# The norm between two layers made inside the first pass of a convolution's input product

## The chip, the cores and the metric

The kernel runs on one core of one Trainium2 chip. The metric is device time in microseconds of one execution, from the first instruction to the last; smaller is better. Engines are named as in the profile: PE is TensorE (matmul), PEld its weight loads, DVE is VectorE, ACT is ScalarE, POOL is GpSimd, SP is SyncE, which here only issues transfers.

## The reference

A network of two layers works on 4096 tokens of width 1024. Layer 0 mixes tokens by a state space model, layer 1 by a short convolution; each is followed by a mixture of experts. What lies around the change is the start of layer 1:

```
hn = modulate(rmsnorm(x, norm1_g[1]), sh1, sc1)       # x * rsqrt(mean(x*x) + eps) * g * (1 + sc1) + sh1
b_g, c_g, v = split(hn @ w_in, 3)                     # w_in 1024 x 3072
u = c_g * v
z = causal depthwise convolution of u, 3 taps
out = (b_g * z) @ w_out
```

The scale and shift belong to a channel, the root mean square to a token.

## The kernel before

The program is a row of phases with a barrier between them. `finish_layer` (tag `c0`) makes the norm between the layers and `conv_in` (tag `conv`) the first product and the convolution; `project` (tag `cout`) and the experts follow. `finish_layer` with tag `c1` makes the final norm at the end.

`finish_layer` takes 32 tiles of 128 tokens. SP loads a tile of x (512 KB, L1845) four deep; ACT squares and sums it (L1878) and takes the root (L1880); DVE takes the reciprocal (L1925), multiplies by it and by the gain (L1930) and adds the shift (L1932), all over 1024 channels with gain and shift broadcast to 128 partitions; PE transposes eight squares of 128 x 128 (L1906); ACT copies them out of PSUM (L1888); POOL stores them into `hnT`, channels by tokens (L1869).

`conv_in` needs products that are as exact as fp32 from the faster fp32r form, so each operand is split into a high part (ACT, a copy that rounds to fp32r) and a low part (DVE, raw minus high), and `product` (L127 to L129) makes three matmuls: weight high by x low, low by high, high by high. Four passes c each take a quarter of the output channels (2 x 128 for each of B, C and V), with their weights held in SBUF. In each pass 8 blocks of 512 tokens follow. A block has two halves m, each with three groups n (C, V, B) of 8 k x 3 matmuls of 128 x 128 by 128 x 512 into a PSUM bank: 48 groups in a pass, 192 in all. SP loads a block of x from `hnT` (2 MB, L1973) as soon as the buffer's block before is done, ACT splits (L2006, two instructions for a block), DVE subtracts (L2070). ACT also copies C out of its bank (L2023), DVE multiplies by V (L2093), applies the taps (L2097 to L2100) and gates with B (L2103), and POOL stores the result to `zT` (L2051). The weights of the next pass (8 transfers of 384 KB, L1970) are split at the start of a pass, ahead of everything else on ACT (L1997) and DVE (L2063). PE's waits are: the weights of the pass, the low part of the block, and for each half m that DVE has read that half's banks (`used`). Six of eight PSUM banks are in use.

All four passes run as hardware loops over pairs of blocks. Each engine's order is the program's; semaphores count up and waits are on counts.

Of the kernel before, what the change touches and what calls it, by code (L numbers as in the profile page):

```python
# [24 lines left out]
F32 = mybir.dt.float32  # L25
# [6 lines left out]
P = 128  # L32
D = 1024
# [1782 lines left out]
def finish_layer(core, ident, tag, layer, x1_dram, mod_dram, gain_src, hnT_dram=None, out=None):  # L1816

    nc = core.nc
    last_layer = out is not None
    W = 8 if last_layer else 4  # L1820
# [4 lines left out]
    tp, t_out, t_st = sem("transposed"), sem("hT_out"), sem("hT_stored", W)  # L1825
    with ExitStack() as ctx:
        sb = lambda name, shape, dt=F32: core.sb(ctx, f"{tag}_{name}", shape, dt)
        sbs = lambda name, n, shape, dt=F32: core.sbs(ctx, f"{tag}_{name}", n, shape, dt)
        gain, shift, scale = sb("gain", [P, D]), sb("shift", [P, D]), sb("scale", [P, D])
        xb, hn = sbs("x", W, [P, D]), sbs("hn", W, [P, D])  # L1830
        junk = sb("junk", [P, D])
        hT = None if last_layer else sbs("hT", W, [P, KD, P])
        eps, stat = sb("eps", [P, 1]), sbs("stat", W, [P, 4])
        pT = None if last_layer else [core.ps(ctx, f"{tag}_pT{s}", [P, KD, P]) for s in range(W)]
        block = ctx.enter_context(nc.Block())
        x1_view = x1_dram[0:T, :].rearrange("(n p) d -> n p d", p=P)
        if last_layer:
            out_view = out.rearrange("b (n p) d -> n p (b d)", p=P)
        else:
            hT_view = hnT_dram.rearrange("(k p) (n f) -> n p k f", p=P, f=P)  # L1840

        @block.sync
        def _(sp):
            def load(n):
                sp.dma_start(xb[n % W][:], x1_view[n]).then_inc(x_ld[n % W], 16)  # L1845
# [4 lines left out]
            if not last_layer:  # L1850
                load_mod(sp, mod_dram, layer + 1, SC1, scale[:], const_ld)
                load_mod(sp, mod_dram, layer + 1, SH1, shift[:], const_ld)
            for n in range(2, W):
                load(n)
            for n in range(NT):
                if n + W < NT:
                    sp.wait_ge(hn_ready, n + 1)
                    load(n + W)

        @block.gpsimd  # L1860
        def _(pool):
            for n in range(NT):
                s = n % W
                if last_layer:
                    pool.wait_ge(hn_ready, n + 1)
                    pool.dma_start(out_view[n], hn[s][:]).then_inc(o_st[s], 16)  # L1866
                else:
                    pool.wait_ge(t_out, n + 1)
                    pool.dma_start(hT_view[n], hT[s][:]).then_inc(t_st[s], 16)  # L1869
            for s in range(W):  # L1870
                pool.wait_ge(o_st[s] if last_layer else t_st[s], 16 * (NT // W))

        @block.scalar
        def _(act):
            def std_of(n):
# [7 lines left out]
            def out_t(n):  # L1883
                s = n % W
                act.wait_ge(tp, n + 1)
                if n >= W:
                    act.wait_ge(t_st[s], 16 * (n // W))
                act.activation(hT[s][:], pT[s][:], ACT.Copy).then_inc(t_out, 1)  # L1888

            act.wait_ge(eps_set, 1)  # L1890
            for n in range(NT + 2):
                if n < NT:
                    std_of(n)
                if n >= 2 and not last_layer:
                    out_t(n - 2)

        if not last_layer:
            @block.tensor
            def _(pe):
                for n in range(NT):  # L1900
                    s = n % W
                    pe.wait_ge(hn_ready, n + 1)
                    if n >= W:
                        pe.wait_ge(t_out, n - W + 1)
                    for k in range(KD):
                        last = pe.transpose(pT[s][:, k, :], hn[s][:, k * P:(k + 1) * P], ident[:])  # L1906
                    last.then_inc(tp, 1)

        @block.vector
        def _(dve):  # L1910
            c = Chain(dve, step)
            dve.memset(eps[:], EPS).then_inc(eps_set, 1)
            dve.wait_ge(const_ld, 16 if last_layer else 48)
            if not last_layer:
                fold_scale(dve, c, gain[:], scale[:])
            stt, tt = dve.scalar_tensor_tensor, dve.tensor_tensor
            for n in range(NT):
                s = n % W
                dve.wait_ge(std, n + 1)
                if n >= W:  # L1920
                    if last_layer:
                        dve.wait_ge(o_st[s], 16 * (n // W))
                    else:
                        dve.wait_ge(tp, n - W + 1)
                c(dve.reciprocal(stat[s][:, 2:3], stat[s][:, 1:2]))  # L1925
                if last_layer:
                    stt(out=hn[s][:], in0=xb[s][:], scalar=stat[s][:, 2:3], in1=gain[:],  # L1927
                        op0=ALU.mult, op1=ALU.mult).then_inc(hn_ready, 1)
                else:
                    c(stt(out=hn[s][:], in0=xb[s][:], scalar=stat[s][:, 2:3], in1=gain[:],  # L1930
                          op0=ALU.mult, op1=ALU.mult))
                    tt(hn[s][:], hn[s][:], shift[:], ALU.add).then_inc(hn_ready, 1)  # L1932
# [4 lines left out]
def conv_in(core, tag, w_in, conv_w, hnT_dram, z_dram):  # L1937
# [5 lines left out]
    TB = T // HALF  # L1943
# [3 lines left out]
    r_ld, r_hi, r_lo = sem("r_loaded", 2), sem("r_hi"), sem("r_split")  # L1947
    mm, c_out, used, step = sem("bank"), sem("c_out"), sem("banks_read"), sem("dve_step")
    z_ready, z_go, z_st = sem("z_ready"), sem("z_stores"), sem("z_stored", 2)
    with ExitStack() as ctx:  # L1950
# [3 lines left out]
        x_raw, x_lo = zip(*[core.raw_low(ctx, f"{tag}_x{s}", [P, KD, HALF]) for s in range(2)])  # L1954
        w_hi, x_hi = sbs("w_hi", 2, [P, KD, 3, W], F32R), sbs("x_hi", 2, [P, KD, HALF], F32R)
        taps = sb("taps", [P, 3, NC_ * MC])
        u = sbs("u", 2, [P, MC, HALF + 2])
        cs = sbs("c", MC, [P, HALF])
        z = sbs("z", MC, [P, HALF])
        pb = [[core.ps(ctx, f"{tag}_p{j}_{m}", [P, HALF]) for j in range(3)] for m in range(MC)]  # L1960
        block = ctx.enter_context(nc.Block())
        w_view = w_in[0].rearrange("(k p) (j c f) -> c p k j f", p=P, j=3, f=W)
        x_view = hnT_dram.rearrange("(k p) (n f) -> n p k f", p=P, f=HALF)
# [3 lines left out]
        def _(sp):  # L1967
# [4 lines left out]
            def load(r, t, s):  # L1972
                sp.dma_start(x_raw[s][:], x_view[bass.ds(t, 1)].squeeze(0)).then_inc(r_ld[s], 16)  # L1973

            sp.dma_start(taps[:], conv_w[0].rearrange("j (c p) -> p j c", p=P), allow_slow_non_contiguous=True) \
              .then_inc(cw_ld, 16)
            weights(0)
            for s in range(2):
                load(0, s, s)
            for c in range(NC_):  # L1980
                if c + 1 < NC_:
                    if c >= 1:
                        sp.wait_ge(mm, 3 * MC * TB * c)
                    weights(c + 1)
                last = c == NC_ - 1
                with sp.Fori(0, TB // 2 - (1 if last else 0)) as i:
                    for s in range(2):
                        b = c * TB + 2 * i + s
                        sp.wait_ge(mm, 3 * MC * (b + 1))
                        load(None, (2 * i + s + 2) % TB, s)  # L1990

        @block.scalar
        def _(act):
            def split_w(c):
                for k in range(KD):
                    act.wait_ge(w_ld[c % 2][k], 16 * (c // 2 + 1))
                    act.activation(w_hi[c % 2][:, k, :, :], w_raw[c % 2][:, k, :, :], ACT.Copy) \  # L1997
                       .then_inc(w_hi_r, 1)

            def split_x(c, i, s):  # L2000
# [172 lines left out]
```

## Time and profile before

| | us |
|---|---|
| median of 3 runs | 7090.4 |
| lowest, highest | 7086.16, 7091.12 |
| the profiled execution, its time | 7087.8 |
| the profiled execution, its span | 7085.8 |

The profiled execution is one execution with the hardware profiler on. Its span is from the first to the last instruction in the trace; its time is 2.0 us longer. Instruction counts, durations and idle times of the profile belong to it alone. The page gives busy shares of the engines over the span, a strip of 40 slices, the queues and the costliest groups of instructions; the trace behind it answers questions on stretches and on single instructions, with times in us from the start of the span. Matmuls are pipelined: a duration of 0.39 us of a 128 x 512 matmul holds its passage through the array, and the rate is read from the distance of two starts.

### The profile page before, as it was taken

To read this page: it belongs to the slowest core of one execution; us is meant where nothing else is said; L and a number is where in the kernel's file an instruction comes from. 1 tells how busy PE (TensorE), PEld (TensorE's weight loads), DVE (VectorE), ACT (ScalarE), POOL (GpSimd) and SP (SyncE) were. 2 spreads that over 40 slices of the span, in tenths; PEclk is the share of its full clock that TensorE was granted. 3 is DMA by queue.
4 is the path that set the end of the run, shared out by engine and by line. 5 is a ranking of instruction groups with operands and counts; after the bars stand their busy time and mean duration, and the time that the engine had idled before them with its cause. 6 is when DMAs were issued, how large, how long until landed. Compare 5 with 4: busy or idle time off the path is not lost. (4 is left out here: it accounts for less than half of the span.)

```text
span 7085.8 us, 90556 instructions
## 1 busy us (share of the span) xinstructions
PE 6435.3 (91%) x30729; PEld 5259.4 (74%) x30730; DVE 3486.6 (49%) x4917; ACT 2114.6 (30%) x3269; POOL 1486.9 (21%) x1278
## 2 busy tenths in 40 slices
PE   6997888799995999999995999998998599999994
PEld 2876766588884888888884888887777488888883
DVE  4435666344336564555646333433544744556554
ACT  1112444222221343343425111111111233344434
POOL 0001221587002222222321000000000322222222
PEclk8998999899997999999995999999998899999997
DMA  6221111444222676676747222221433465677766
GB/s 202 66 85 45 60 51 46 153 145 142 83 80 101 187 225 178 201 213 201 213 131 269 74 94 97 84 87 66 155 130 116 134 193 165 187 215 238 221 201 246
DMA packets 502953, 1024.21 MB, mean 145 GB/s; under 512 B 62526, under 2 KB 140350, under 8 KB 501834
## 3 DMA queue, kind: packets, MB, share of 16 engines
q1 hardware_dynamic: 395604, 740.36, 30.7%
q0 software_dynamic: 74336, 265.88, 14.5%
q10 hardware_dynamic: 32920, 16.80, 0.8%
q8 instruction: 50, 0.82, 0.0%
q14 instruction: 43, 0.35, 0.0%
HBM read 784.34 MB, written 238.60 MB: 144 GB/s over the span
## 5 line engine op out<-in xcount | busy, mean ns | idle before, releaser
L127 PE MATMUL conv_p<-conv_x_lo,conv_w_hi 128*128 128x512 f32 x1536 | 598.7, 390 | 33.0 <-DVE conv_x_lo L2070 33.0
L128 PE MATMUL conv_p<-conv_x_hi,conv_w_lo 128*128 128x512 f32 x1536 | 598.5, 390 | 0.0
L129 PE MATMUL conv_p<-conv_x_hi,conv_w_hi 128*128 128x512 f32 x1536 | 598.5, 390 | 0.0
L1758 DVE SCALAR_TENSOR_TENSOR m_o<-m_pO,m_weight_of,m_gate 128x512 f32<-128x512 f32 x320 | 237.8, 747 | 723.9 <-PE m_pO L1478 404.4
L1725 DVE TENSOR_TENSOR m_w_lo<-m_w_raw,m_w_hi 128x1024 fp32r<-128x1024 f32 x496 | 577.6, 1214 | 0.0
L1533 ACT ACTIVATE m_xT_hi<-m_pX 128x512 fp32r<-128x512 f32 x320 | 191.6, 599 | 1151.9 <-PE m_pB L129 994.2
L127 PE MATMUL m_pA<-m_w_lo,m_xT_hi 128*128 128x512 f32 x1280 | 517.2, 404 | 5.7 <-DVE m_xT_lo L1736 5.7
L1474 PE MATMUL m_pO<-m_w_lo,m_hT_hi 128*128 128x512 f32 x1280 | 512.8, 401 | 0.5 <-ACT m_hT_hi L1538 0.5
L1521 ACT ACTIVATE m_w_hi<-m_w_raw 128x1024 fp32r<-128x1024 f32 x512 | 505.3, 1053 | 0.0
L129 PE MATMUL m_pA<-m_w_hi,m_xT_hi 128*128 128x512 f32 x1280 | 502.9, 393 | 0.0
L128 PE MATMUL m_pA<-m_w_hi,m_xT_lo 128*128 128x512 f32 x1280 | 500.2, 391 | 0.0
L1474 PE MATMUL m_pO<-m_w_hi,m_hT_hi 128*128 128x512 f32 x1280 | 498.9, 390 | 0.0
L127 PE MATMUL m_pB<-m_w_lo,m_xT_hi 128*128 128x512 f32 x1280 | 498.1, 389 | 0.0
L129 PE MATMUL m_pB<-m_w_hi,m_xT_hi 128*128 128x512 f32 x1280 | 498.0, 389 | 0.0
L128 PE MATMUL m_pB<-m_w_hi,m_xT_lo 128*128 128x512 f32 x1280 | 497.9, 389 | 0.0
L1383 POOL COPY m_gather_now<-m_gather_of 128x1 int32 (+1 forms) x164 | 186.7, 1138 | 1162.6 <-DMA x<-m_o,m_scatter_now 874.2
L127 PE MATMUL glu_pM<-glu_w_lo,glu_sT_hi 128*128 128x512 f32 x1024 | 405.9, 396 | 12.1 <-DVE glu_w_lo L1111 12.1
L129 PE MATMUL glu_pM<-glu_w_hi,glu_sT_hi 128*128 128x512 f32 x1024 | 401.6, 392 | 0.0
L128 PE MATMUL glu_pM<-glu_w_hi,glu_sT_lo 128*128 128x512 f32 x1024 | 401.5, 392 | 0.0
L127 PEld LDWEIGHTS conv_p<-conv_x_lo,conv_w_hi 128*128 128x128 f32 x1536 | 289.0, 188 | 93.5 <-issue 33.4
L1731 DVE TENSOR_TENSOR m_w_lo<-m_w_raw,m_w_hi 128x1024 fp32r<-128x1024 f32 x256 | 306.2, 1218 | 86.3 <-issue 65.6
L1478 PE MATMUL m_pO<-m_w_hi,m_hT_lo 128*128 128x512 f32 x1280 | 342.1, 389 | 0.0
(346 smaller groups left out, 13001.3 us busy)
## 6 DMA issues: line engine op xcount, KB each, us to landing
m_w_raw<-in_moe_w_dram SPq DMA_DIRECT2D x384, 1024.0 KB, 7.2
conv_x_raw<-hnT SPq DMA_DIRECT2D x32, 2048.0 KB, 9.3
c_x<-x SPq DMA_DIRECT2D x64, 512.0 KB, 7.5
mod_w<-in_ada_w_dram SPq DMA_DIRECT2D x12, 2048.0 KB, 7.9
glu_ada<-in_ada_w_dram POOLq DMA_DIRECT2D x96, 256.0 KB, 3.2
a_x<-in_x_dram SPq DMA_DIRECT2D x32, 512.0 KB, 3.5
u<-a_stage POOLq DMA_DIRECT2D x4, 4096.0 KB, 19.1
s_u<-u SPq DMA_DIRECT2D x64, 256.0 KB, 2.6
```

The costliest lines, as they stand in the source:

```text
L127: pe.matmul(out, lh, rl, start=start, stop=False)
L128: pe.matmul(out, ll, rh, start=False, stop=False)
L129: return pe.matmul(out, lh, rh, start=False, stop=stop)
L1383: pool.tensor_copy(gx[:], gidx[:, bass.ds(t, 1)]).then_inc(gi_ready, 1)
L1474: pe.matmul(pO[:, n, :], hT_hi[:, k, :], w[:, n, k, :], start=k == 0 and w is w2_low, stop=False)
L1478: last = pe.matmul(pO[:, n, :], hT_lo[:, k, :], w2_high[:, n, k, :], start=False, stop=k == KF - 1)
L1521: act.activation(W13[s][2][:, m, k:k + 2, :], W13[s][0][:, m, k:k + 2, :], ACT.Copy).then_inc(w13_hi, 1)
L1533: act.activation(xT_hi[:, 4 * q:4 * q + 4, :], pX[:, 4 * q:4 * q + 4, :], ACT.Copy).then_inc(xt_hi, 1)
L1725: tt(W13[s][1][:, m, k:k + 2, :], W13[s][0][:, m, k:k + 2, :], W13[s][2][:, m, k:k + 2, :].bitcast(F32), ALU.subtract).then_inc(w13_lo, 1)
L1731: tt(w2_low[:, n, k:k + 2, :], w2_raw[:, n, k:k + 2, :], w2_high[:, n, k:k + 2, :].bitcast(F32), ALU.subtract).then_inc(w2_lo, 1)
L1758: dve.scalar_tensor_tensor(out=ob[:, n, :], in0=pO[:, n, :], scalar=wslot[:, bass.ds(tile_, 1)], in1=gate2[:, n, :], op0=ALU.mult, op1=ALU ...
```

## The change

`finish_layer` keeps only the final norm, under the name `final_norm`; its work at the end of the program is as before. The phase `c0` and the tensor `hnT` are gone. `conv_in` now gets x, the gain and the row of modulation, and its pass 0 is written out without a loop:

- SP loads the four 128-token tiles of block 0, then the weights of pass 0. For each block b it waits until the block is transposed, loads the tiles of block b + 1 into the same four buffers, waits for the low parts, and stores high and low part (2 x 2 MB) to two tensors in DRAM. The weights of pass 1 go out behind the stores of block 0.
- Gain, scale, shift (1024 numbers each, laid out 8 to a partition) and taps are loaded from POOL's queue; DVE folds the gain once.
- ACT makes square sum and root of a tile; DVE takes the reciprocal and multiplies the tile in place (`scaled`), without gain and shift.
- PE transposes 4 squares of 128 x 128 into one of the two PSUM banks that were free (`turned`), for block 0 all eight k ahead of the products, for block b + 1 two k behind each of the first four groups of block b.
- ACT reads the bank with an affine copy, with gain and shift as its per-partition operands, into `xt` (`x_high`), then rounds it into the high part; DVE subtracts (`x_low`).
- Passes 1 to 3 load high and low part of a block ready (two transfers of 2 MB instead of one), and ACT and DVE split no x there. PE waits for the loads themselves.

The core of the diff:

```diff
+            def load(t, s):
+                for part, dst in zip(hT_view, (x_hi[s], x_lo[s])):
+                    sp.dma_start(dst[:].bitcast(F32), part[bass.ds(t, 1)].squeeze(0)).then_inc(r_ld[s], 16)
+            for j in range(TPB):
+                sp.dma_start(rows[j][:], x_view[j]).then_inc(n_ld[j], 16)
             weights(0)
+            for b in range(TB):
+                sp.wait_ge(t_psum, KD * (b + 1))
+                if b + 1 < TB:
+                    for j in range(TPB):
+                        sp.dma_start(rows[j][:], x_view[TPB * (b + 1) + j]).then_inc(n_ld[j], 16)
+                sp.wait_ge(r_lo, KD * (b + 1))
+                for part, src in zip(hT_view, (x_hi[b % 2], x_lo[b % 2])):
+                    sp.dma_start(part[b], src[:].bitcast(F32)).then_inc(r_st[b % 2], 16)
+                if b == 0:
+                    weights(1)
             for s in range(2):
-                load(0, s, s)
+                sp.wait_ge(r_st[s], 32 * (TB // 2))
+            for s in range(2):
+                sp.wait_ge(mm, GROUPS * (TB - 1 + s))
+                load(s, s)
...
+            def x_high(b, k):
+                n = KD * b + k
+                act.wait_ge(t_psum, n + 1)
+                if n >= 2:
+                    act.wait_ge(r_lo, n - 1)
+                act.activation(xt[n % 2][:], pT[n % 2][:], ACT.Identity, scale=gains[:, 0, k:k + 1],
+                               bias=gains[:, 2, k:k + 1]).then_inc(t_out, 1)
+                act.wait_ge(t_out, n + 1)
...
+                act.activation(x_hi[b % 2][:, k, :], xt[n % 2][:], ACT.Copy).then_inc(r_hi, 1)
...
+            for n in range(TPB):
+                std_of(n)
+            act.wait_ge(gain_ready, 1)
+            for k in range(KD):
+                x_high(0, k)
+                w_high(0, k)
+            for n in range(TPB, 2 * TPB):
+                std_of(n)
+            for b in range(TB):
+                c_copy(b, 0)
+                if b + 1 < TB:
+                    for k in range(6):
+                        x_high(b + 1, k)
+                c_copy(b, 1)
+                if b + 1 < TB:
+                    for k in range(6, KD):
+                        x_high(b + 1, k)
+                if b + 2 < TB:
+                    for n in range(TPB * (b + 2), TPB * (b + 3)):
+                        std_of(n)
...
+            def turned(b, k):
+                n = KD * b + k
+                if k == 0:
+                    pe.wait_ge(n_ready, TPB * (b + 1))
+                if n >= 2:
+                    pe.wait_ge(t_out, n - 1)
+                for j in range(TPB):
+                    last = pe.transpose(pT[n % 2][:, j * P:(j + 1) * P], rows[j][:, k * P:(k + 1) * P], ident[:])
+                last.then_inc(t_psum, 1)
...
+            for k in range(KD):
+                turned(0, k)
+            for b in range(TB):
+                pe.wait_ge(r_lo, KD * (b + 1)) if b else None
+                for m in range(MC):
+                    pe.wait_ge(used, MC * b + 1 + m)
+                    for n in range(3):
+                        group(0, b % 2, m, n, b + m + n == 0)
+                        if b + 1 < TB and 3 * m + n < 4:
+                            turned(b + 1, 2 * (3 * m + n))
+                            turned(b + 1, 2 * (3 * m + n) + 1)
...
+            for b in range(TB):
+                q = lambda m: Chain(dve, step, base_of(0) + 1 + (b * MC + m) * per)
+                more = b + 1 < TB
+                for k in range(2 if more else 0):
+                    x_low(b + 1, k)
+                taps_of(0, b, b % 2, 0, q(0))
+                for k in range(2, 4 if more else 2):
+                    x_low(b + 1, k)
+                gated(b, 0)
+                for k in range(4, KD if more else 4):
+                    x_low(b + 1, k)
+                taps_of(0, b, b % 2, 1, q(1))
+                gated(b, 1)
+                if b + 2 < TB:
+                    for n in range(TPB * (b + 2), TPB * (b + 3)):
+                        scaled(n)
+                if b == 1:
+                    for k in range(KD):
+                        w_low(1, k)
```

`scaled(n)` is a reciprocal of 128 x 1 and a `tensor_scalar` multiply of 128 x 1024 in place, with the reciprocal as its per-partition operand. `taps_of` and `gated` hold the instructions of L2093 to L2103. `group` holds the loop over k of `product`.

## Rows read from the trace of the kernel before

**Rows 1.** The profile's page, part 1: engine, busy us, share of span, instructions.
```profile
PE 6435.3 (91%) x30729; PEld 5259.4 (74%) x30730; DVE 3486.6 (49%) x4917; ACT 2114.6 (30%) x3269; POOL 1486.9 (21%) x1278
```

**Rows 2.** Table of stretches around the change; columns as its first line says.
```profile
core 0: us, PE busy (x) PEld busy (x) DVE busy (x) ACT busy (x) POOL busy (x), PEclk, DMA share, GB/s
3757.40:3866.00 108.60, 62.98 (x256) 50.19 (x256) 84.36 (x98) 77.20 (x129) 28.52 (x32) 0.50 0.87 324
3866.00:3891.10 25.10, 0.00 (x0) 0.00 (x0) 12.16 (x10) 10.90 (x11) 0.00 (x0) 0.50 1.00 331
3891.10:4154.90 263.80, 263.78 (x1153) 218.20 (x1154) 98.77 (x120) 44.60 (x40) 8.14 (x15) 0.99 0.23 79
4154.90:4938.20 783.30, 783.30 (x3457) 648.43 (x3455) 286.33 (x353) 124.75 (x110) 25.95 (x48) 1.00 0.25 86
```

**Rows 3.** Groups by line from 3745 to 3900: busy us, mean ns | idle before.
```profile
L1932 DVE TENSOR_TENSOR c_hn<-c_hn,c_shift 128x1024 f32<-128x1024 f32 x32 | 39.2, 1225 | 1.1
L1869 POOL DMA_DIRECT2D hnT<-c_hT x32 | 28.5, 891 | 82.6 <-ACT c_hT L1888 82.6
L1925 DVE RECIPROCAL c_stat<-c_stat 128x1 f32<-128x1 f32 x32 | 5.0, 157 | 2.3 <-ACT c_stat L1880 2.3
```

**Rows 4.** The same table, the first products of pass 0 alone.
```profile
3891.10:3896.40 5.30, 5.28 (x12) 4.18 (x13) 4.62 (x5) 4.41 (x6) 0.00 (x0) 0.50 1.08 380
```

**Rows 5.** Timeline of the norm phase's start.
```profile
3761.12 1.06 ACT L1878 ACTIVATE c_junk<-c_x 128x1024 f32<-128x1024 f32 x1 [21.04 <-DMA c_x<-x]
3762.08 0.19 ACT L1878 ACTIVATION_READ_ACCUMULATOR c_junk<-c_x 128x1 f32 x1
...
3763.58 0.29 ACT L1880 ACTIVATE c_stat<-c_stat,c_eps 128x1 f32<-128x1 f32 x1
...
3771.21 1.97 PE L1906 MATMUL c_pT<-ident,c_hn 128*128 128x128 f32 x8 [25.63 <-DVE c_hn L1932]
```

**Rows 6.** Transfers by line: count, KB of each, median us to landing.
```profile
conv_x_raw<-hnT SPq DMA_DIRECT2D x32, 2048.0 KB, 9.3
...
u<-a_stage POOLq DMA_DIRECT2D x4, 4096.0 KB, 19.1
...
conv_taps<-in_conv_w_dram SPq DMA_DIRECT2D x1, 12.0 KB, 3.6
```

**Rows 7.** Single lines of DVE: ns min/median/max, first and last start us.
```profile
L1068 DVE TENSOR_SCALAR cout_gate<-cout_gate x1: 693/693/693, 4961.1 to 4961.1; 128x1024 f32<-128x1024 f32 x1
...
L2097 DVE TENSOR_SCALAR conv_z<-conv_u,conv_taps x64: 485/486/490, 3905.9 to 4933.9; 128x512 f32<-128x512 f32 x64
L2070 DVE TENSOR_TENSOR conv_x_lo<-conv_x_raw,conv_x_hi x64: 2282/2288/2294, 3886.5 to 4886.8; 128x2048 fp32r<-128x2048 f32 x64
...
L2103 DVE TENSOR_TENSOR conv_z<-conv_z,conv_p x64: 686/687/689, 3910.3 to 4938.5; 128x512 f32<-128x512 f32 x64
```

**Rows 8.** ACT's groups by form, whole span: rounding copies from SBUF.
```profile
L1140 ACT ACTIVATE cout_sT_hi<-cout_src 128x512 fp32r<-128x512 f32 x64 | 36.8, 622 | 36.2 <-DMA cout_src<-zT 33.3 <-issue 2.8
L1997 ACT ACTIVATE conv_w_hi<-conv_w_raw 128x768 fp32r<-128x768 f32 x32 | 27.1, 846 | 62.5 <-DMA conv_w_raw<-in_conv_w_in_dram 61.9
```

**Rows 9.** Timeline of PE in the expert layer, eight transposes between products.
```profile
3689.39 1.03 PE L1435 MATMUL m_pX<-ident,m_rows 128*128 128x128 f32 x8
3690.18 0.48 PE L1474 MATMUL m_pO<-m_w_lo,m_hT_hi 128*128 128x512 f32 x1
3690.50 0.40 PE L1474 MATMUL m_pO<-m_w_hi,m_hT_hi 128*128 128x512 f32 x1
```

**Rows 10.** Table of stretches, 45 us of the expert layer.
```profile
3690.00:3735.00 45.00, 43.70 (x206) 36.05 (x205) 14.58 (x22) 9.12 (x15) 7.98 (x12) 1.00 0.26 59
```

**Rows 11.** Timeline of DVE in the first block of pass 1: its first gating.
```profile
4183.16 0.69 DVE L2103 TENSOR_TENSOR conv_z<-conv_z,conv_p 128x512 f32<-128x512 f32 x1
```

**Rows 12.** Timeline of PE in `cout`: a wait of 1.1 us, then slow products.
```profile
5105.95 1.98 PE L1222 MATMUL cout_pH<-cout_router,cout_hT 128*128 128x36 f32 x16 [1.11 <-ACT cout_hT L1158]
...
5108.84 0.63 PE L127 MATMUL cout_pM<-cout_w_lo,cout_sT_hi 128*128 128x512 f32 x1
```

More of the change, by code:

```diff
@@ L1849, in _ @@
             sp.dma_start(gain[:], row(gain_src, 0, D)).then_inc(const_ld, 16)
-            if not last_layer:
-                load_mod(sp, mod_dram, layer + 1, SC1, scale[:], const_ld)
-                load_mod(sp, mod_dram, layer + 1, SH1, shift[:], const_ld)
             for n in range(2, W):
                 load(n)
[L1855 to L1858, printed above, removed]
+            for n in range(NT - W):
+                sp.wait_ge(hn_ready, n + 1)
+                load(n + W)
         @block.gpsimd
@@ L1881, in std_of @@
                    .then_inc(std, 1)
[L1883 to L1907, printed above, removed]
         @block.vector
@@ L1912, in _ @@
             dve.memset(eps[:], EPS).then_inc(eps_set, 1)
[L1913 to L1916, printed above, removed]
+            dve.wait_ge(const_ld, 16)
             for n in range(NT):
@@ L1920, in _, with conv_in @@
                 if n >= W:
[L1921 to L1924, printed above, removed]
+                    dve.wait_ge(o_st[s], 16 * (n // W))
                 c(dve.reciprocal(stat[s][:, 2:3], stat[s][:, 1:2]))
[L1926 to L1937, printed above, removed]
+                dve.scalar_tensor_tensor(out=hn[s][:], in0=xb[s][:], scalar=stat[s][:, 2:3], in1=gain[:],
+                                         op0=ALU.mult, op1=ALU.mult).then_inc(hn_ready, 1)
+def conv_in(core, ident, tag, x_dram, norm_g, mod_row, w_in, conv_w, hT_dram, z_dram):
     nc = core.nc
@@ L1942, in conv_in @@
     W = P * MC
-    TB = T // HALF
+    TB, TPB = T // HALF, HALF // P
+    GROUPS = 3 * MC
     sem = lambda name, n=None: core.sem(f"{tag}_{name}", n)
@@ new lines, in group @@
+            def group(c, s, m, n, first=False):
+                j, cols = (1, 2, 0)[n], slice(m * P, (m + 1) * P)
+                for k in range(KD):
+                    if first:
+                        pe.wait_ge(r_lo, k + 1)
+                        pe.wait_ge(w_split, k + 1)
+                    last = product(pe, pb[m][n][:], (w_hi[c % 2][:, k, j, cols], w_lo[c % 2][:, k, j, cols]),
+                                   (x_hi[s][:, k, :], x_lo[s][:, k, :]), k == 0, k == KD - 1)
+                last.then_inc(mm, 1)
@@ new lines, in _ @@
+            for k in range(KD):
+                turned(0, k)
[8 more added lines that the diff above has]
+                            turned(b + 1, 2 * (3 * m + n) + 1)
@@ L2029, in _ @@
+            for c in range(1, NC_):
                 pe.wait_ge(w_split, KD * (c + 1))
```

235 lines of the change are left out of this document (121 added, 114 removed).

## The prediction

> **What bounds the kernel now.** I read the summary first, then the table of stretches, then the timelines at the joints. TensorE is busy for 91% of the span, so the kernel ends when TensorE's stream ends, and what can be won lies where that stream has a hole or runs slowly [rows 1]. The stretches show one such hole around the change. From 3757.4 us to 3891.1 no product of the convolution runs: the norm phase takes 108.6 us (256 transposes at the low clock, 0.50), the start of `conv_in` another 25.1 us with TensorE idle. From 3891.1 to 4938.2 TensorE is busy for 1047.1 us of 1047.1 [rows 2]. The norm phase keeps DVE busy for 84.4 of its 108.6 us; the adding of the shift alone takes 1225 ns for each of 32 tiles [rows 2, 3]. Downstream nothing changes, so each microsecond by which the convolution's last product moves is one of the end.
>
> In the convolution four passes of 8 blocks make 48 groups of 24 matmuls each. Passes 1 to 3 take 783.3 us, so a group takes 783.3/144 = 5.44 us and a block of six 32.6 us; pass 0 takes 263.8 us, 2.5 us more, because its first 12 matmuls run at the low clock (0.50, which is 1.2 GHz) with starts 5.3/12, over 0.43 us apart, where a later one takes 783.3/3456 = 0.23 [rows 2, 4].
>
> **What is removed.** The norm phase as a whole (TensorE transposes, ScalarE's copies, the 32 stores, the constants broadcast to 128 partitions), one phase change, and the splits of x in passes 1 to 3 (two instructions of 128x2048 each of ScalarE and DVE in a block; 2.29 us for one of DVE [rows 7]). ScalarE and DVE are idle most of the time there [rows 2], so those splits give nothing by themselves. The gain is the hole of 3891.1 - 3757.4 = 133.7 us, less what the new start needs, less what is put into TensorE's stream.
>
> **The new start.** The phase begins at 3757.4 as before. ScalarE began on the first 512 KB of x 3.7 us into the phase (that is how long its landing took), and the transfers of that time moved 324 GB/s, thus 1.6 us for each 512 KB [rows 2, 5]. The four tiles of block 0 are there by 3765.9, now ahead of all else on SP's queue. ScalarE has the first deviation at 3763.9, table load included, and takes 1.06 + 0.19 + 0.29 us for each further one [rows 5]: the fourth at 3768.4. The small loads of gain, scale and shift are moved to POOL's queue; three issues of at most 0.9 us, the price of a 1024-run issue there [rows 3], and a landing of 3.6 us, that of the taps [rows 6], put them at 3764, hidden behind the norm. DVE scales the fourth tile by 3769.4, four transposes at 0.25 us each (1.97 us for eight at the low clock [rows 5]) end at 3770.4. Now ScalarE is the bound: for each of the 8 k it makes the affine copy and the high part (0.62 each, a copy of the same length) and a weight's high part (0.85) [rows 8], with gaps 2.2 us. TensorE stands with all eight transposes before its first product, and the last of them waits for the affine copy of k = 5, at 3782.1; products begin at 3783.1. The first 12 run at 0.43 us (3788.2), the other 12 at 0.23 us, ending at 3790.9; the last low part of a weight is ready at 3789.1 and costs nothing.
>
> Then a **bubble**. The rows of block 1 can be loaded only when block 0 is transposed (3783.1): they land from 3786.8 to 3791.6. ScalarE, free at 3788.1, has their fourth deviation at 3794.3, DVE the scaled tile at 3795.3, and TensorE's next instruction, the first transpose of block 1, waits for that from 3790.9: 4.4 us. Behind it in the same queue stand the other five groups of block 0. After it I charge one more slow start, 2.4 us. Block 0 ends at 3795.3 + 5 x 5.44 + 3.5 (its transposes, below) + 2.4 = 3828.4.
>
> **Transposes in the stream.** A block's 32 come in four slots of eight, and in the expert layer eight transposes stand between products just so: they start at 3689.39, the next product at 3690.18 and its follower 0.32 us on instead of 0.23 [rows 9]. That is 0.79 + 0.09 = 0.88 us for a slot and 3.5 us for a block, at full clock (1.00 over 45 us that hold two such slots [rows 10]). The bounds are 0.79 and, at the low clock, 1.97 us [rows 5]. Seven blocks cost 24.6 us, 3.5 of them already in block 0. TensorE's wait for a bank of k - 2 costs nothing, as ScalarE empties it in 0.6 us and a group lies between.
>
> **Does the norm keep up in pass 0?** A block has 36.1 us. ScalarE needs 8 x 1.3 + 4 x 1.55 + 2 x 0.6 = 17.8 us, DVE 8 x 0.69 [rows 7] + 4 x 1.0 + 2 x 3.7 (the gap-free run of taps and gating) = 16.9 us; neither is the bound by amount. The order leaves two places to look at. At a block's start T, DVE must finish the last gating (T + 1.0, from its 0.69 us and start 0.3 us after the last product [rows 7]), then scale four tiles before the transposes at T + 5.44. A scaling is a reciprocal of 0.16 us and a TENSOR_SCALAR with a pointer over 1024 elements. No row has that one. Bounds are 0.69 us (same length, constant operand) and 1.23 us (TENSOR_TENSOR, same length); the row of the same kind has 486 ns for 512 elements, and the 1024-element constant form has 693 [rows 3, 7], which makes 486 + 267 = 0.75 us, near the lower end. Then four end at T + 5.0, with 0.4 us to spare. The rows of the next block are issued two groups before T and land by T - 2, free of the stores of the block before. The second place is the end: the last transposes are at T + 25.4, and 0.6 + 2 x 1.3 + 0.7 us later the block's parts are ready, 7 us early.
>
> By the Trainium skill, VectorE: DVE Perf Modes, section Mode 2×_2P, a single-source operation on SBUF makes two fp32 results a cycle and tensor_tensor can't; 1225 against 693 ns in the rows agrees. If a pointer scalar lost that mode, each block would start 1.5 us late, the case given below from rows alone.
>
> **Stores and loads.** The two parts (4 MB a block) are stored on SP's queue behind the next rows; 4 MB on a queue landed in 19.1 us once [rows 6], against 36 us of a block. From pass 1 on two transfers of 2 MB replace one, which landed in 9.3 us [rows 6]: at most 18.6 us of the 32.6 that lie between issue and use. The seam of pass 0 and 1 is tighter. The parts of block 7 are stored from 29 us after block 6 begins, done 19.1 us later, 12 us into block 7; the load of block 8 behind it ends at most 18.6 us on, 2 us before use. At the seams where weights(2) and weights(3) are loaded, ScalarE waits for them and the copies of C queue behind. Before, pass 0 ended at 4154.9 and the first gating of the new pass at 4183.9, 29.0 us into a block of 32.6 [rows 2, 11]. Now 2 MB more stand ahead (at most +7.3 us, the 9.3 of such a load [rows 6] less some 2 for its reaction), but the splits of x ahead of the first gating are gone, between 4.6 us (two of 2.29) and 5.4: about 31 us. No wait, with 1.6 us to spare.
>
> **Sum.** Block 0 ends at 3828.4; blocks 1 to 6 take 6 x 36.16 = 217.0, block 7 32.6: 4078.0. Passes 1 to 3, 783.3: 4861.3 instead of 4938.2, 76.9 us sooner. The profiled execution has a span of 7085.8 and a time of 7087.8 us, thus 7008.9 and 7010.9; the median of the three runs, 7090.4, lies 2.6 us above it, and I predict 7013.5, rounded **7014 us**.
>
> **Rivals.** (1) *The norm comes late at each block*: with 1.23 us for the scaling the fourth is ready at T + 6.9, a wait of 1.5 us in six blocks, and where TensorE had waited 1.1 us once and then ran 16 small matmuls, its clock fell and the next nine product starts were 0.35 to 0.43 us apart instead of 0.23, some 1.8 us lost (one of the nine stands in the rows, with 0.63 us for 0.39) [rows 12]. 6 x 3.3 = 20 us: **7034**. For it: the margin is only 0.4 us; against it: the 486 ns row. 15%. (2) *A shorter start*: no bubble and no second slow start, 6.8 us, and the cheaper slot, 2.5 us: **7005**. 5%. (3) *No change, the norm isn't hidden after all*: if each of seven blocks waited 11 us, the gain of 76.9 would be gone: **7090**. Nothing in the amounts above speaks for that, only the handshakes of four engines. 3%. (4) *Slower, through the clock*: the many short waits between slots keep TensorE at 1.2 GHz in pass 0. A group then takes 24 x 0.427 = 10.2 us, 4.8 more; from 16 of the 48 groups on the change loses, and with all 48 it costs 230 us: **7244** at the worst, some 7110 with 20. For it: the clock that fell after a single short wait [rows 12]; against it: full clock with such slots in the expert layer [rows 10]. 5%. The forecast has 70%.
>
> (5) *Reading the code*: pass 0 is now written out, 2816 matmuls and weight loads of TensorE without a loop, and reading them might stall, which no row of a written-out stretch of this length can rule out. By the Trainium skill, Runtime: NRT & Kernel Launch, section Instruction fetch mechanics, a straight stream is fetched ahead in blocks of 256 instructions and it is taken branches that stall; that would cost nothing here. The trace shows no loss at the old loop's branches either (783.3 of 783.3 us busy [rows 2]). Were each of the eight blocks to wait once for a small landing, 3.6 us [rows 6], and then lose 1.8 us to the clock [rows 12], 43 us would go: **7057**, which I give 2%.
>
> **Chances and range.** Faster by over 0.2% (14 us, about what a measurement of this kernel can tell from no change): 0.70 + 0.15 + 0.05 + 0.02, thus 0.92; same 0.03; slower 0.05. The range reaches from rival (2), less 3 us, to rival (1) and some 10 us for a late seam or dearer slots: 7001 to 7045.
>
> **What would show it.** Right: first product near 3783, one wait of TensorE of 3 to 6 us behind the first group for DVE's scaled rows and none in blocks 2 to 7, a scaling of 0.75 us, slots of 0.88 us, pass 0 over near 4078, passes 1 to 3 in 783 us, granted clock 1.00 from block 1 on. Wrong: waits of the transposes at each block, a product waiting for loaded parts in pass 1, a clock under 1.00 inside pass 0, or TensorE idle for "issue".

## The result and the profile after

| | before | after |
|---|---|---|
| median, us | 7089.17 (4 runs) | 7015.77 (4 runs) |
| lowest, highest | 7086.16, 7091.12 | 7012.22, 7019.38 |
| profiled execution, span | 7085.8 | 7013.7 |

The ratio is 0.9897, 95% interval 0.9885 to 0.9908: 73.4 us less, where 76.9 were forecast, and 7015.8 where 7014 was predicted. (The forecast started from 7090.4, the median of three of the four runs.)

First the table of stretches of the changed kernel, from the end of its first block: start:end, length, busy time of PE, PEld, DVE, ACT and POOL with counts, granted clock, DMA share, GB/s.

```profile
3831.40:4048.70 217.30, 217.30 (x1057) 182.09 (x1057) 102.15 (x176) 104.78 (x176) 6.51 (x12) 1.00 0.51 187
4081.00:4864.70 783.70, 783.70 (x3459) 648.98 (x3457) 185.22 (x307) 41.91 (x64) 26.04 (x48) 1.00 0.40 147
```

The first line is blocks 1 to 6 with the norm in them, the second passes 1 to 3. TensorE is busy for the whole of both at clock 1.00; the second answers the last of [rows 2], with ScalarE's busy time down from 124.8 to 41.9 us and DVE's from 286 to 185, and takes as long as before. The list of TensorE's waits over both confirms it: from 3786 to 4870 it has two entries (columns: waiting instruction, releaser, us in total, times, longest).

```profile
PE conv_pT L2035 <- DVE conv_rows L2104: 5.6, 1, 5.6
PE conv_pT L2035 <- ACT conv_xt L1980: 0.9, 1, 0.9
```

Only the first lies between products; the second is the last wait of the prologue. The timeline of TensorE there (start us, duration, engine, line, instruction, idle before):

```profile
3785.63 1.11 PE L2035 MATMUL conv_pT<-ident,conv_rows 128*128 128x128 f32 x4 [0.94 <-ACT conv_xt L1980]
3786.40 0.78 PE L127 MATMUL conv_p<-conv_x_lo,conv_w_hi 128*128 128x512 f32 x1
...
3792.86 0.39 PE L129 MATMUL conv_p<-conv_x_hi,conv_w_hi 128*128 128x512 f32 x1
3798.89 1.97 PE L2035 MATMUL conv_pT<-ident,conv_rows 128*128 128x128 f32 x8 [5.64 <-DVE conv_rows L2104]
...
3836.67 0.39 PE L129 MATMUL conv_p<-conv_x_hi,conv_w_hi 128*128 128x512 f32 x1
3836.90 1.03 PE L2035 MATMUL conv_pT<-ident,conv_rows 128*128 128x128 f32 x8
3837.69 0.48 PE L127 MATMUL conv_p<-conv_x_lo,conv_w_hi 128*128 128x512 f32 x1
3838.01 0.40 PE L128 MATMUL conv_p<-conv_x_hi,conv_w_lo 128*128 128x512 f32 x1
```

The bubble stands behind the first group, and a slot of eight transposes looks in its times exactly as in the expert layer [rows 9]. ScalarE in the prologue, one k:

```profile
3770.76 1.06 ACT L1971 ACTIVATE conv_junk<-conv_rows 128x1024 f32<-128x1024 f32 x1 [1.52 <-DMA conv_rows<-x]
...
3776.57 0.76 ACT L1980 ACTIVATE conv_xt<-conv_pT,conv_gains 128x512 f32<-128x512 f32 x1
3777.36 0.63 ACT L1986 ACTIVATE conv_x_hi<-conv_xt 128x512 fp32r<-128x512 f32 x1
3777.90 0.83 ACT L1966 ACTIVATE conv_w_hi<-conv_w_raw 128x768 fp32r<-128x768 f32 x1
```

Its period is 2.06 us a k; the first line is the square sum of the fourth tile, which came late.

**Where the time went.** The phase starts at 3757.43 before and at 3759.72 after; over all profiled runs of this study with the new `conv_in` it starts between 3756.3 and 3760.9, though nothing ahead of it was changed. So the convolution is best measured from its phase's start. The last gating starts at 4938.49 before and 4864.94 after, 1181.1 and 1105.2 us into the stretch: 75.8 us less (forecast 76.9). The later start took 2.3 us back, and what follows the last product is 1.4 us longer. That part too moves without a cause in the change: from the last k's first product to the end it took 2148.3 us before, 2149.6 after, and between 2149.8 and 2153.1 in the profiled runs below that change nothing in it; `parts_alone`, which has the old norm phase, is one of them with 2151.5.

In all experiments the numbers "products begin" and "last k" (the start of the last product of line 127) are counted in us from the start of the phase; for the changed kernel they are 26.7 and 1104.3.

### The profile page after: what moved, and what is told of

Same layout as the page of the kernel before. It is cut to its first block and busy times, and to the rows that moved or that the text cites. A ratio compares the mean times of both kernels' runs of the same rounds, so it can differ in the third digit from the quotient of the medians.

```text
span 7013.7 us, 90561 instructions
## 1 busy us (share of the span) xinstructions
PE 6407.3 (91%) x30729; PEld 5236.7 (75%) x30730; DVE 3326.9 (47%) x4885; ACT 2051.1 (29%) x3301; POOL 1448.3 (21%) x1250
## 5 line engine op out<-in xcount | busy, mean ns | idle before, releaser
L129 PEld LDWEIGHTS conv_p<-conv_x_hi,conv_w_hi 128*128 128x128 f32 x1536 | 288.9, 188 | 59.9
```

What stands on the lines that cost most here:

```text
L129: return pe.matmul(out, lh, rh, start=False, stop=stop)
```

## The experiments

### One part alone: ready parts without the hidden norm

SP stores both parts in pass 0 (first hunk) and loads them in passes 1 to 3 (second hunk, with the condition under which x is still split); pass 0 splits x as before, only the others no longer do; `finish_layer` stays.

```diff
+            for b in range(TB):
+                s = b % 2
+                sp.wait_ge(r_lo, 2 * b + 2)
+                for part, src in zip(hT_view, (x_hi[s], x_lo[s])):
+                    sp.dma_start(part[b], src[:].bitcast(F32)).then_inc(r_st[s], 16)
...
+                        parts((2 * i + s + 2) % TB, s)
...
-                        if not (c == NC_ - 1 and last and s == 1):
+                        if c == 0 and not (last and s == 1):
                             split_x(c, *at(i, s, 1))
```

> One part of the change alone: the norm stays a phase of its own as in the kernel before, pass 0 of the convolution splits x as before and stores both parts, passes 1 to 3 load them ready. Theory (the whole gain is the hidden norm): TensorE was busy all through those passes, so nothing moves, 7089 +- 4 us. Rival (the ready parts relieve ScalarE and DVE and carry some of the gain): under 7080. Rival (4 MB for a block and the stores cost something): over 7095.

Measured: 7091.25 us against 7088.66, ratio 1.0004 (0.9995 to 1.0013). The table of its stretches:

```profile
3866.00:3891.50 25.50, 0.00 (x0) 0.00 (x0) 12.15 (x10) 10.86 (x11) 0.00 (x0) 0.50 1.01 335
3891.50:4155.00 263.50, 263.48 (x1153) 218.00 (x1154) 94.36 (x118) 41.02 (x38) 8.15 (x15) 0.99 0.57 214
4155.00:4938.00 783.00, 783.00 (x3456) 648.31 (x3455) 185.12 (x307) 41.91 (x64) 25.95 (x48) 1.00 0.40 147
```

DVE is relieved by the same 100 us as in the changed kernel and the pass takes the same 783 us. The last k starts 1180.1 us after the norm phase's start in both traces. The ready parts bring nothing and cost nothing here. What they are for is room: with them passes 1 to 3 need neither norm nor transposes. The other half, a hidden norm whose result is split again in every pass, was not run.

### What the transposes cost in the stream

```diff
-                for j in range(TPB):
+                for j in list(range(TPB)) * (2 if b else 1):
                     last = pe.transpose(pT[n % 2][:, j * P:(j + 1) * P], rows[j][:, k * P:(k + 1) * P], ident[:])
```

> The changed kernel with every transpose of blocks 1 to 7 made twice into the same place (the same values). Theory (the transposes stand in TensorE's stream at full clock and cost what they take): 28 slots of eight more at 0.79 us, 22 us, time near 7038, clock 1.00 in blocks 1 to 7, a block of 39.4 us. Rival (part of their time is covered or paid for by other waits): under 7030. Rival (longer stretches of transposes bring the clock down): over 7060, with clocks under 1.00.

Measured: 7039.65 us, ratio 0.9930 (0.9913 to 0.9946), last k at 1129.3: 25.0 us more. The gatings of blocks 1, 2 and 3 in its timeline and in the changed kernel's are 39.71 and 36.21 us apart, so a block pays 3.50 us more, 0.88 a slot, not the 0.79 I had put on the added ones. A doubled slot at full clock:

```profile
3838.34 1.91 PE L2035 MATMUL conv_pT<-ident,conv_rows 128*128 128x128 f32 x16
3840.00 0.48 PE L127 MATMUL conv_p<-conv_x_lo,conv_w_hi 128*128 128x512 f32 x1
```

From the slot's first start to the next product are 1.66 us, for a single one 0.79. The clock stayed at 1.00 from 3831 to 4070. So the transposes are paid in full, 24.5 us in the change, and stretches of sixteen of them don't bring the clock down.

### The margin at each block's start

```diff
-                dve.tensor_scalar(rows[s][:], rows[s][:], stat[s][:, 2:3], None, ALU.mult).then_inc(n_ready, 1)
+                if n < 2 * TPB:
+                    dve.tensor_scalar(rows[s][:], rows[s][:], stat[s][:, 2:3], None, ALU.mult).then_inc(n_ready, 1)
+                else:
+                    dve.tensor_tensor(rows[s][:], rows[s][:], stat[s][:, 2:3].broadcast_to([P, D]), ALU.mult).then_inc(n_ready, 1)
```

> The changed kernel with the rows of blocks 2 to 7 scaled by a TENSOR_TENSOR against the broadcast reciprocal (1.23 us instead of 0.75). Theory (0.8 us of margin before the first transposes of a block): four scalings end 1.9 us later, 1.1 us behind the first group, six waits of 1.1 us, and up to 1.8 us of clock behind each: 7 to 17 us more, 7022 to 7033. Rival (the margin isn't where I read it, the rows aren't waited for): no wait and 7016.

Measured: 7025.61 us (7020.12 to 7027.76), ratio 0.9907 (0.9890 to 0.9924), last k at 1111.8: 7.5 us more. Its waits from 3830 on, all there are, and one of them with what follows:

```profile
PE conv_pT L2035 <- DVE conv_rows L2107: 5.9, 6, 1.0
```

```profile
3839.35 1.09 PE L2035 MATMUL conv_pT<-ident,conv_rows 128*128 128x128 f32 x8 [0.98 <-DVE conv_rows L2107]
3840.19 0.48 PE L127 MATMUL conv_p<-conv_x_lo,conv_w_hi 128*128 128x512 f32 x1
3840.51 0.39 PE L128 MATMUL conv_p<-conv_x_hi,conv_w_lo 128*128 128x512 f32 x1
```

Six waits as rival (1) of the prediction had them, but each cheaper: 0.98 us, and behind it the products run at 0.39 us. The clock was 1.00 over all six (3839 to 4052), nothing is lost to it. The rival's mechanism is real and its price was nearly three times too high: 7.5 us instead of 20. Compared by medians the run is 9.8 us above the changed kernel; its phase also began 1.2 us later.

### The margin at the seams

```diff
                     sp.wait_ge(mm, GROUPS * TB * c)
+                    if c == 2:
+                        sp.wait_ge(extra, 16 * TPB)
+                    for j in range(TPB):
+                        sp.dma_start(rows[j][:], x_view[j]).then_inc(extra, 16)
                     weights(c + 1)
```

> The changed kernel with 2 MB of x more loaded (into the row buffers, unused) ahead of the weights at the beginning of passes 1 and 2. Theory (the gating of the pass's first block has 2.9 us to spare before TensorE needs its banks): the weights land 5.5 to 7.3 us later, TensorE waits 2.6 to 4.4 us at each of the two seams and loses up to 1.8 us of clock: 5 to 12 us more, 7021 to 7028. Rival (the transfers share the queues and the weights aren't held up): 7016.

Measured: 7021.23 us, ratio 0.9903 (0.9887 to 0.9920), last k at 1112.1: 7.7 us more. The changed kernel's last gating minus that of pass 0 is 783.3 us; here the passes take 7.8 more. Waits of TensorE from 3830 on, and the second of them:

```profile
PE conv_p L127 <- DVEq L2136: 4.4, 2, 2.7
```

```profile
4378.90 0.80 PE L127 MATMUL conv_p<-conv_x_lo,conv_w_hi 128*128 128x512 f32 x1 [2.75 <-DVEq L2136]
4379.49 0.63 PE L128 MATMUL conv_p<-conv_x_hi,conv_w_lo 128*128 128x512 f32 x1
```

1.6 us at the first seam with no loss of clock (1.00), 2.75 at the second, and the clock falls: it is 0.51 over the next 6.2 us, fourteen product starts are 0.42 us or more apart, and some 3 us are lost, where the expectation had at most 1.8. In the changed kernel the first gating of pass 1 is

```profile
4110.03 0.69 DVE L2128 TENSOR_TENSOR conv_z<-conv_z,conv_p 128x512 f32<-128x512 f32 x1
```

and TensorE needs its banks at some 4113.9, so the room is 3 us. With 6 instead of 4 MB ahead of the weights they came 5.0 us later and the two seams cost 7.8 us, 4.4 of them waiting; the change's 4 MB cost nothing.

### Is the bubble a wait that can be moved?

```diff
-                        if b + 1 < TB and 3 * m + n < 4:
-                            turned(b + 1, 2 * (3 * m + n))
-                            turned(b + 1, 2 * (3 * m + n) + 1)
+                        at_ = 3 * m + n - (1 if b == 0 else 0)
+                        if b + 1 < TB and 0 <= at_ < 4:
+                            turned(b + 1, 2 * at_)
+                            turned(b + 1, 2 * at_ + 1)
```

> Theory (bubble): the changed kernel loses 5.6 us where the first transposes of block 1 wait for DVE's scaled rows behind the first group, and 1.8 us more to the low clock behind it. Moving block 1's four slots of transposes from behind groups 1 to 4 to behind groups 2 to 5 gives the norm 5.4 us more: the wait shrinks to 0.3 us or less, the slow restart goes, the convolution's last product ends some 7 us sooner after the phase's start (1098 us instead of 1105), time near 7009. Rival (the wait only moves): the parts of block 1 come late for its first product instead, a wait of about as much stands at the start of block 1, time near 7016.

Measured: 7009.66 us (7009.12 to 7012.12), ratio 0.9889 (0.9874 to 0.9904), last k at 1098.1: 6.3 us sooner. There is no wait behind the first group any more, and the slow products behind it are gone. A part is given back one block on: the rows of block 2 are now loaded one group later, and their first transposes wait.

```profile
PE conv_pT L2035 <- DVE conv_rows L2105: 0.8, 1, 0.8
```

A wait did move, as the rival said, but for another tile and at a seventh of the price. The two kernels' times, 7009.7 and, at other times, 7015.8 and 7017.9 for the changed one, are 6.1 and 8.3 us apart, which fits the 6.3 us of the traces.

### What bounds the start

Three edits on top of `slots_later`. In `both_early` two high parts of the weights are made ahead of the first affine copy, the others still one behind each k:

```diff
+            for k in range(2):
+                w_high(0, k)
             act.wait_ge(gain_ready, 1)
             for k in range(KD):
                 x_high(0, k)
-                w_high(0, k)
+                if k + 2 < KD:
+                    w_high(0, k + 2)
...
```

> As slots_later, and the high parts of two weights are made while ScalarE waits for the first transposes. Theory (the start is bound by ScalarE's row of 2.06 us for each k): 1.6 us more, products and everything behind them sooner, 1096 us from the phase's start to the last product, time near 7007. Rival (the start is bound by when the weights land): ScalarE waits for them before its first affine copy and nothing or less than nothing is won, 7009 to 7011.

Measured: 7012.36 us, ratio 0.9891 (0.9876 to 0.9906); products begin at 27.0 (26.9 in `slots_later`), last k at 1099.0. Nothing was won, and not for the rival's reason: its two weight copies fill the gap before the first affine copy (at 3772.33, 1.56 us, ahead of an affine copy at 3774.69 that waits for TensorE). The bound of the start is the affine copy of k = 5, as the prediction has it, and this order leaves five weight copies between the first and that one. My expectation had forgotten that. In `start_order` they stand where they are out of its way, and DVE's low parts follow the same order:

```diff
+            for what, k in (("w", 0), ("w", 1), ("x", 0), ("x", 1), ("w", 2), ("x", 2), ("x", 3), ("w", 3), ("x", 4), ("x", 5), ("w", 4),
+                            ("x", 6), ("w", 5), ("x", 7), ("w", 6), ("w", 7)):
+                if what == "x" and k == 0:
+                    act.wait_ge(gain_ready, 1)
+                (x_high if what == "x" else w_high)(0, k)
```

> slots_later, with the high parts of the weights (ScalarE) and their low parts (DVE) put in another order in the start: two ahead of the first affine copy, the others behind each second part of x. Theory (the first product waits for the affine copy of k = 5, which stood behind five weight copies and now stands behind two and one): products start 2 us sooner after the phase's start than the 26.8 us of slots_later, some 24.9, and the first group ends at least 1 us sooner; time 7008. Rival (the first group then waits for its weights and ends when it did): products sooner, end of the first group and time as in slots_later, 7010.

Measured: 7008.22 us (7006.99 to 7010.60), ratio 0.9885 (0.9868 to 0.9901); products begin at 24.7, 2.2 us sooner, last k at 1096.6, 1.5 us sooner. The rest went where the rival had put all of it:

```profile
PE conv_p L127 <- DVE conv_w_lo L2098: 1.0, 1, 1.0
```

In `taps_late` only the load of the taps is held back:

```diff
+            pool.wait_ge(t_psum, 1)
             pool.dma_start(taps[:], conv_w[0].rearrange("j (c p) -> p j c", p=P), allow_slow_non_contiguous=True) \
...
```

> slots_later, with the load of the taps (3072 pieces of 4 bytes) held back on POOL's queue until the first transposes are done. Theory (the small pieces of gains and taps take turns with the rows on the DMA engines and delay them): the fourth tile of block 0 is there 1 us or more sooner than 11.1 us into the phase and products begin as much sooner, 1 to 2 us, time 7008. Rival (the rows are delayed by the weights queued behind them): the fourth tile comes when it came, 7010.

Measured: 7009.46 us, ratio 0.9887 (0.9871 to 0.9904); ScalarE begins the fourth tile at 9.7 instead of 11.2 us, products begin at 25.7 instead of 26.9, last k at 1098.0, that of `slots_later`: 1.2 us won in the start, and the wait for block 2's rows grew from 0.8 to 1.4 us.

```profile
3829.34 1.09 PE L2035 MATMUL conv_pT<-ident,conv_rows 128*128 128x128 f32 x8 [1.39 <-DVE conv_rows L2106]
```

The other half microsecond went in the first group. In this trace its first eight product starts are 0.42 us or more apart, in `slots_later`'s only five, so it ends 0.6 us sooner and not 1.2, and the longer wait takes just that. How many products run slowly there is not set by any of the edits: in the eleven profiled runs with the new `conv_in` it is between 2 and 12 (2 in `start_order`, 10 in `all_three`), which moves the end of the group by up to 1.7 us.

> slots_later, start_order and taps_late in one. Theory: the savings in the start add up, 1.2 + 1 to 2 us, less a wait of 1.4 us for block 2's rows at block 1: convolution's last product 1096 us after the phase's start, time 7007, the lowest of all. Rival (what the start wins is given back at the first group's end or at block 1): 7010 as slots_later.

Measured: 7008.02 us (7005.41 to 7010.58), ratio 0.9884 (0.9868 to 0.9901), products at 24.7, last k at 1096.8: no sooner than `start_order`. The two savings don't add. The fourth tile is there 1.0 us sooner, but DVE's first scaling stands behind the folding of the gains, and these landed no sooner, 10.1 us into the phase in both:

```profile
3768.94 0.17 DVE L2138 SCALAR_TENSOR_TENSOR conv_gains<-conv_gains 128x8 f32<-128x8 f32 x1 [9.92 <-DMA conv_gains<-mod]
```

From there four scalings of 0.87 us follow without a gap, and the tile is no longer what is waited for. In `taps_late` the gains had landed at 8.9 instead of 9.9 us, and its saving of 1.2 us is theirs as much as the tile's. It is the fastest median of the study by 0.2 us, which is no difference.

> The changed kernel unaltered, on the same chip as the two above, so that they can be compared with it: 7016 +- 3 us, the last product of the convolution 1105 us after the phase's start; by the theory of the bubble slots_later and its kin stand 6 us under it.

Measured: 7017.91 us (7016.28 to 7018.43), ratio 0.9898 (0.9881 to 0.9914), products at 26.8, last k at 1104.5. Against it on the same chip `start_order` and `all_three` are 9.7 and 9.9 us faster, all runs of the one below all runs of the other; 7.9 and 7.6 of these stand in the convolution of the traces.

### The affine copy

```diff
-                act.activation(xt[n % 2][:], pT[n % 2][:], ACT.Identity, scale=gains[:, 0, k:k + 1],
-                               bias=gains[:, 2, k:k + 1]).then_inc(t_out, 1)
+                act.activation(xt[n % 2][:], pT[n % 2][:], ACT.Copy).then_inc(t_out, 1)
```

> The affine copy out of PSUM is a plain copy; gain, scale and shift of this norm are left out of the computation. Theory (the per-partition operands make it 0.77 us long instead of 0.60): it takes 0.60, ScalarE's row for a k in the start falls from 2.06 to 1.9 us, and the first product starts some 1 us sooner. Rival (the length comes from reading beside TensorE's writes or from the low clock there): it stays near 0.77.

One run: 7049.6 us, but other values reach the second layer's router, so the time of the whole says nothing here. In the trace the copy is:

```profile
L1980 ACT ACTIVATE conv_xt<-conv_pT x64: 577/582/598, 3772.6 to 4036.4; 128x512 f32<-128x512 f32 x64
```

and in the changed kernel:

```profile
L1980 ACT ACTIVATE conv_xt<-conv_pT,conv_gains x64: 759/766/780, 3774.5 to 4039.0; 128x512 f32<-128x512 f32 x64
```

The same place, the same bank, the same clock: the affine form takes 184 ns more. (The run changes the function, Identity to Copy, together with its two operands; which of these costs the time it can't tell.) ScalarE's period for a k falls from 2.06 to 1.88 us and products begin at 25.6 instead of 26.7.

## Why the prediction was right

Counted from the phase's start (3757.4 predicted, 3759.7 in the trace after; a block's end is its last gating's start less 0.3 us):

| step | predicted | measured |
|---|---|---|
| fourth tile's deviation ready | 11.0 | 12.5 |
| products begin | 25.7 | 26.7 |
| end of the first group | 33.5 | 33.4 |
| length of the first group | 7.8 | 6.7 |
| bubble | 4.4 | 5.6 |
| end of block 0 | 71.0 | 71.7 |
| a block with four slots | 36.16 | 36.21 |
| end of pass 0 | 320.6 | 321.6 |
| passes 1 to 3 | 783.3 | 783.3 |
| end of the last product | 1103.9 | 1104.9 |

**The hole and what fills it.** The gain is the hidden norm alone, which `parts_alone` shows by the absence of any without it. The four terms taken from rows of the same work (the norm's own instructions, the slot of eight transposes from the expert layer, a group, passes 1 to 3) held to a few per cent.

**The transposes.** 0.88 us a slot, shown twice, by the block's period and by the doubled slots.

**The scaling.** 0.75 us (752 to 757 ns in 32), as forecast. The prediction added 267 ns for the second half of the row to the 486 ns of the half-length one, and none of its rows shows that slope; the runs give 754 - 486 = 268 ns. Four end 4.6 us after the block's start instead of 5.0, since each follows the one before in 0.87 us rather than 1.0; the margin was 0.8 us and not 0.4. With the length of the two-source form, the dearer bound, waits appeared, so the row chosen decided between no wait and six.

**The start: terms that were mis-sized, and evened out by luck.** ScalarE got to the fourth tile 1.5 us later than I had worked out. I had divided by the rate of the norm phase, 324 GB/s, but in the 11.1 us from 3759.7 the DMA engines moved 224 GB/s at a busy share of 0.93:

```profile
3759.70:3770.80 11.10, 0.00 (x0) 0.00 (x0) 1.24 (x6) 5.54 (x11) 4.24 (x4) 0.50 0.93 224
```

Beside the rows stood the gains and taps, 6144 numbers of 4 bytes that lie apart. What such pieces do to the DMA engines can be seen in the trace of the kernel before, where SP loads the 3072 of the taps first in the phase: in these 2 us they are nearly all that is moved (2801 of 2803 packets are under 512 bytes), the engines are 78% busy, and 7 GB/s pass (columns as in [rows 2]).

```profile
3866.00:3868.00 2.00, 0.00 (x0) 0.00 (x0) 0.00 (x0) 0.00 (x0) 0.00 (x0) 0.50 0.78 7
```

With the taps held back (`taps_late`) the same 11.1 us moved 263 GB/s instead of 226 in `slots_later`, and the fourth tile came 1.5 us sooner. The gains themselves landed 9.8 us into the phase and not at 6.6, and DVE's first scaling waited for them in its queue; that cost nothing only because three scalings of 0.87 us were done just when the fourth deviation came. It is a tie and not a margin: in `transposes_twice` and `seam_load` the gains landed at 10.4 us and the products began 0.5 us later. I called these loads hidden, at the 3.6 us of one load of taps ahead of all else on SP's queue, where the loads on POOL's queue took 6.8 to 8.7 us, and had not asked what they do to the others'. The affine copy took 0.77 for 0.62 us, yet the period was 2.06 for 2.2 us, as ScalarE starts an independent copy some 0.1 us before the one ahead of it has ended. Five periods of 0.14 us less took a part of the delay back, and the first product came 1.0 us late. The first group then gave that back. The prediction had charged it with 12 slow starts, as in the kernel before; the clock rose after five:

```profile
3788.25 0.63 PE L128 MATMUL conv_p<-conv_x_hi,conv_w_lo 128*128 128x512 f32 x1
3788.68 0.47 PE L129 MATMUL conv_p<-conv_x_hi,conv_w_hi 128*128 128x512 f32 x1
3788.99 0.40 PE L127 MATMUL conv_p<-conv_x_lo,conv_w_hi 128*128 128x512 f32 x1
```

That the group ended at 33.4 us for 33.5 predicted is luck, since how many products run slowly there moves from one profiled run to another. In the total, chance is larger than what is left to explain: the phase started 2.3 us later and what follows the convolution took 1.4 us longer, while the median before was 1.2 us lower than the one the forecast used. What the forecast can be held to is the convolution itself: 1103.9 us predicted, 1104.9 measured.

**The bubble** was named with its place and releaser; it was 1.2 us longer (rows asked for 1.4 us later, at 27.1 for 25.7, since the last transposes of block 0 were done later, and scaled as much later), and behind it four product starts at 0.43 us and a slow slot cost 1.8 us, 2.4 predicted. `slots_later` shows both as one removable cost.

**Rivals.** (1) has the right mechanism at a wrong price: the waits were 0.98 us for 1.5, and the clock did not fall after them. (2) would have needed the edit of `slots_later`. (3) and (4) did not come; the clock in blocks 1 to 7 was 1.00 even with doubled slots. (5): TensorE shows no idle time for "issue" in the written-out pass; by the Trainium skill, Runtime: NRT & Kernel Launch, section Instruction fetch mechanics, a straight stream is fetched ahead, and this trace, with 217.3 of 217.3 us busy in code that never repeats, agrees.

**The seams.** The wait predicted as absent by 1.6 us was absent by 3: the 2 MB more held the weights up by 5.2 us (ScalarE's first copy of them at 15.8 us into the pass instead of 10.7) and not by 7.3, and the splits that left the pass's start took 5.4 us off DVE.

The prediction says that pass 0 before took 2.5 us more than one of the others; it is 263.8 - 261.1 = 2.7. The forecast did not use the figure.

What no run here settles is why the phase starts up to 4.6 us apart in kernels that are the same until then.

## What to carry to other kernels

A phase whose TensorE work is small and whose span is mostly another engine's (here DVE, busy for 84 of 109 us) is best put inside a neighbour whose TensorE is full: the price is its own TensorE time, here 0.88 us for eight transposes, and a new start, here 26.7 us and a bubble of 5.6 where the old phases had taken 133.7. The sum is then decided at the joints, so list each engine's queue for the first and the last block by hand: who waits for the first tile, who for the buffer of the second. Place moved work one group later in the first block than in the others, where its inputs come from a pipe that is still filling.

## What the runs showed of the hardware

- ScalarE's copy of 128x512 out of PSUM takes 582 ns as a copy and 766 ns with a scale and a bias for each partition.
- The load of 3072 numbers of 4 bytes that lie apart kept the DMA engines 78% busy at 7 GB/s (before, 3866 to 3868). Two such loads' worth beside 2 MB of rows: 224 GB/s at a DMA busy share of 0.93, against 325 over the first 11 us of the old norm phase, which has none; with half of them held back 263 (`taps_late`). On POOL's queue they landed after 6.8 to 8.7 us, where the taps, first on SP's queue, took 3.6 [rows 6].
- TensorE's granted clock stayed at 1.00 through waits of 0.8, 0.98 (six times), 1.4 and 1.6 us between products, and fell after waits of 2.75 and 5.6 us. Before the change it had fallen after 1.1 us followed by 16 small matmuls [rows 12].
- After the 32 transposes of the start, the first products ran slowly (0.42 us or more from start to start, 0.23 later) for 2 to 12 starts in eleven profiled runs, five in the changed kernel.
